# Input projection and paged sample attention as one stage of a hybrid decoder step

## The chip, the cores and the metric

One Trainium2 chip, one of its cores. The kernel is written engine by engine: TensorE (PE) multiplies, VectorE (DVE) and ScalarE (ACT) do elementwise work and reductions, GpSimd (POOL) does elementwise work and issues DMAs, SyncE (SP) issues DMAs. The program orders them by semaphores alone. The metric is the device time of one execution in microseconds (us); below 0.3% a difference can't be told from none.

## What is computed

One layer of a hybrid trunk in float32, for a prompt of 1040 tokens (16 meta tokens and 1024) and for 8 sample sequences of 4 new tokens each, with 4096 cached positions per sequence in 32 pages of 128.

```python
def mixer_inputs(h, ...):
    z = rms_norm(h, norm_w) @ w_in                       # 1024 -> 3600 columns
    dq, dk, dv, dg, gq, gk, gv, gg, ga = split(z)        # 512 512 512 512 256 256 512 512 16
    dq, dk = rms_norm(dq), rms_norm(dk)                  # per group of 64
    lg = log_sigmoid(ga @ gla_wa2 + gla_ba) / 16

def diff_attn_sample(...):                               # 8 sequences, 4 heads, 2 maps of 64
    kp, vp = cache_k[page_table], cache_v[page_table]    # 32 pages of 128 x 512 each
    a = softmax([q . kp + bias, q . k_new + bias])
    p = a[map 0] - lam * a[map 1]
    return p @ [vp, v_new]

def merge_out(...):
    mix = [rms_norm(o_d) * 0.8 * silu(dg), rms_norm(o_g) * silu(gg)]
    return h + mix @ w_out
```

Between the two stand causal differential attention over the prompt and a chunked gated linear attention (GLA), whose chunks of 128 tokens pass a state on.

## The kernel before

The tokens lie in 9 tiles: 8 of 128 rows and a last one of 64 rows, which holds the prompt's last 16 rows and the 32 sample rows. The program runs in five stages, each a block of its own with a barrier at its end, so that no instruction of one runs beside another stage.

**Projection** (lines 108 to 747). x is normed, turned by the PE and split into two fp32r parts (`xTh`, `xTl`), the weights likewise (`wh`, `wl`, on ACT and DVE); every product is three matmuls (hi*hi, lo*hi, hi*lo) over 8 slices of 128 input rows, 24 matmuls in a row. Columns are taken in 15 blocks of up to 256. For q, k, v, gv and both gates (dg, gg) a unit is one token tile: x is stationary, 256 weight columns move (`z_nat`, line 512), 108 units. For gq and gk (`z_turned`, line 524) the weights are stationary and 384, 384 or 320 tokens move: 12 units. q and k are then normed and turned; all of qT, kT, gqT, gkT, bT stay in SBUF. Values and gates go to DRAM.

**Paged sample attention** (lines 749 to 1148). For each sequence, 8 groups of 4 pages. SP loads keys into 4 slots (`load_keys`, line 817), POOL values into 8 (`load_values`, line 843): a page is 256 KB, fetched by a row number read from SBUF. The PE turns the keys 128x128 (line 925), ACT and DVE copy them out of PSUM, and the PE forms scores with a stationary of 32 queries' columns and 128 keys moving, four pages side by side in four column tiles of the array (line 940). Softmax, a turn of the probabilities (line 959), and products with 512 value columns, again in four column tiles (line 969).

**Prompt attention** (lines 1152 to 1636), then **GLA** (1640 to 2074), then the **output projection** (2077 to 2191), which again splits in two parts and adds the residual.

In GLA the loop over tiles is a ring of engines. For tile i+2 POOL forms exponents (`exponents`, lines 1894 to 1934) into one of two slots of `dd`, ACT takes exponentials (`decays`, line 1837), DVE multiplies (`factors`), the PE multiplies (line 1750), DVE masks and updates the state, ACT copies the outputs and takes norms, DVE applies norm and gate (`norm`, line 2048), the PE turns the result and ACT stores it to `mixT` (`mixed`, line 1873). POOL multiplies the gates by the norm weight (`gate`, line 1949), which needs only their load:

```python
for i in range(TILES):          # POOL
    if i + 2 < TILES:
        exponents(pool, linked, i + 2)
    gate(i)
```

ACT runs `decays(i + 2)`, `out(i)`, `turned_k(i + 1)`, `mixed(i - 1)` in this order.

## Time and profile before

| | us |
|---|---|
| median of 3 runs (1261.86, 1263.21, 1266.35) | 1263.21 |
| span of the profiled execution, first to last instruction | 1259.8 |
| until the first product of the projection | 18.65 |
| projection, to 418.5 | 399.85 |
| paged sample attention, to 816 | 397.5 |
| prompt attention, to 1021 | 205 |
| GLA and the start of the output projection, to 1178 | 157 |
| rest of the output projection | 81.8 |

The page gives no time of its own for the profiled execution besides its span; the span is 3.4 us under the median of the runs. "Busy" of the PE is modelled for pipelined matmuls, so the distance between starts tells the pace better than the length of one.

### The profile page before, as it was taken

What the parts mean: (1) busy time and instruction counts of PE and PEld (TensorE: products, weight loads), DVE (VectorE), ACT (ScalarE), POOL (GpSimd) and SP (SyncE); (2) the same over time, 40 slices, a digit from 0 to 9 for tenths busy, and PEclk for the clock granted to TensorE, in tenths of its full rate; (3) what the DMA queues carried; (4) which work ended last, traced back from release to release, by engine and by line L of the source; (5) the groups of instructions that cost most, each with busy time, mean ns of one, the idle gap of its engine ahead of it and who ended that gap; (6) DMA issues with size and microseconds to landing.
All of it is one profiled execution on the core that took longest, in us unless ns stands there. A gap on an engine that the chain in (4) does not pass through costs nothing. (4 is left out here: it accounts for less than half of the span.)

```text
span 1259.8 us, 27242 instructions
## 1 busy us (share of the span) xinstructions
PE 1038.3 (82%) x9055; PEld 868.5 (69%) x9055; DVE 584.6 (46%) x1430; ACT 490.0 (39%) x1383; POOL 254.2 (20%) x399
## 2 busy tenths in 40 slices
PE   4999999999999487879878887467788836777998
PEld 4999999997999466556655654155667625664886
DVE  4755522302222134443443443277878458868221
ACT  5644314613424223333333432156767345533110
POOL 0000000000000222343434341222211159800000
PEclk9999999999999799999999998558999967787999
DMA  5312332212111699999999999530000052102221
GB/s 169 93 38 95 106 122 80 82 34 76 53 49 49 215 386 338 385 387 387 387 387 387 387 387 169 148 111 9 17 10 13 1 175 74 51 26 69 97 89 60
DMA packets 106820, 195.21 MB, mean 155 GB/s; under 512 B 14406, under 2 KB 48652, under 8 KB 106732
## 3 DMA queue, kind: packets, MB, share of 16 engines
q1 hardware_dynamic: 85716, 126.03, 30.8%
q0 software_dynamic: 20480, 67.13, 14.3%
q8 instruction: 54, 0.88, 0.3%
q10 hardware_dynamic: 536, 0.89, 0.2%
q14 instruction: 34, 0.28, 0.1%
HBM read 174.41 MB, written 19.60 MB: 154 GB/s over the span
## 5 line engine op out<-in xcount | busy, mean ns | idle before, releaser
L843 POOL DMA_DIRECT2D vraw<-in_cache_v x256 | 137.6, 537 | 667.7 <-issue 663.8
L512 PE MATMUL pz<-wh,xTh 128*128 128x256 f32 (+1 forms) x864 | 248.7, 288 | 0.0
L512 PE MATMUL pz<-wh,xTl 128*128 128x256 f32 (+1 forms) x864 | 244.3, 283 | 0.0
L512 PE MATMUL pz<-wl,xTh 128*128 128x256 f32 (+1 forms) x864 | 244.2, 283 | 0.0
L925 PE MATMUL pk<-ident,kraw 128*128 128x128 f32 x1024 | 136.7, 291 | 57.0 <-DMA kraw<-in_cache_k 54.0
L925 PEld LDWEIGHTS pk<-ident,kraw 128*128 128x128 f32 x1024 | 121.8, 150 | 70.9 <-DMA kraw<-in_cache_k 62.0
L863 DVE COPY kt<-pk 128x512 f32<-128x512 f32 x128 | 82.9, 687 | 183.1 <-PE pk L925 182.1
L512 PEld LDWEIGHTS pz<-wh,xTh 128*128 128x128 f32 (+1 forms) x864 | 160.6, 186 | 1.6 <-issue 1.2
L512 PEld LDWEIGHTS pz<-wh,xTl 128*128 128x128 f32 (+1 forms) x864 | 160.7, 186 | 0.0
L512 PEld LDWEIGHTS pz<-wl,xTh 128*128 128x128 f32 (+1 forms) x864 | 160.5, 186 | 0.0
L643 DVE SCALAR_TENSOR_TENSOR wl<-wraw,nw,wh 128x256 fp32r<-128x256 f32 x112 | 52.3, 482 | 117.1 <-ACT wh L358 116.2
L861 ACT ACTIVATE kt<-pk 128x512 f32<-128x512 f32 x128 | 70.3, 595 | 80.0 <-PE pk L925 80.0
L1374 PE MATMUL pS<-ks,qs 128*128 128x512 f32 (+3 forms) x288 | 78.6, 426 | 10.0 <-DVE bl L1613 10.0
L969 PE MATMUL po<-vraw,pT 128*32 128x512 f32 x512 | 74.0, 652 | 11.3 <-DMA vraw<-in_cache_v 10.8
L940 PEld LDWEIGHTS psc<-kt,qq 128*32 128x32 f32 x2048 | 56.3, 110 | 39.1 <-issue 31.1
L940 PE MATMUL psc<-kt,qq 128*32 128x128 f32 x2048 | 72.2, 277 | 2.3 <-DVE kt L863 0.9
L1410 PE MATMUL pO<-vd,pT_b 128*128 128x128 f32 (+2 forms) x360 | 49.1, 310 | 22.8 <-ACT pT_b L1478 21.9
L1410 PEld LDWEIGHTS pO<-vd,pT_b 128*128 128x128 f32 (+2 forms) x360 | 39.7, 187 | 34.0 <-ACT pT_b L1478 22.9
L358 ACT ACTIVATE wh<-wraw,nw 128x256 fp32r<-128x256 f32 (+1 forms) x120 | 53.8, 484 | 23.8 <-PE pz L512 18.0
L871 ACT ACTIVATE sc<-psc 128x128 f32<-128x128 f32 x64 | 17.7, 277 | 115.4 <-PE psc L940 115.4
L2188 PE MATMUL pY<-woh,mh 128*128 128x512 f32 (+1 forms) x144 | 57.3, 398 | 5.7 <-DVE wol L2164 5.7
L1750 PE MATMUL pA<-ff 64*128 64x128 f32 (+1 forms) x264 | 27.5, 369 | 39.4 <-DVE at L2011 24.4
(241 smaller groups left out, 1857.5 us busy)
## 6 DMA issues: line engine op xcount, KB each, us to landing
kraw<-in_cache_k SPq DMA_DIRECT2D x256, 256.0 KB, 9.6
vraw<-in_cache_v POOLq DMA_DIRECT2D x256, 256.0 KB, 5.7
wraw<-in_w_in SPq DMA_DIRECT2D x14, 1024.0 KB, 5.6
out<-nat SPq DMA_DIRECT2D x32, 128.0 KB, 1.8
xb<-in_x_prompt SPq DMA_DIRECT2D x7, 512.0 KB, 3.6
xr<-in_x_prompt SPq DMA_DIRECT2D x7, 512.0 KB, 3.5
out<-xr SPq DMA_DIRECT2D x7, 512.0 KB, 2.6
val_d<-nat SPq DMA_DIRECT2D x16, 128.0 KB, 1.8
```

The lines of the kernel that those rows point to most:

```text
L358: act.activation(wh[:, c % 2, k, 0:n], wraw[:, c % 2, k, 0:n], ACT.Copy, scale=nw[:, k:k + 1])\
L512: ins = pe.matmul(z_at(u)[0:r, 0:CB], a[:, k, P * i:P * i + r], b[:, c % 2, k, :], start=(n == 0), stop=(n == 3 * KT - 1))
L643: dve.scalar_tensor_tensor(out=wl[:, c % 2, k, 0:n], in0=wraw[:, c % 2, k, 0:n], scalar=nw[:, k:k + 1], in1=wh[:, c % 2, k, 0:n].bitcast(F32),
L843: pool.dma_start(vraw[:, g % VR, n, :], cache_v.rearrange("a n p h d -> (a n) p (h d)")[bass.ds(page, 1)] .rearrange("o p c -> (o p) c")). ...
L861: ins = eng.activation(kt[:, g % 2, h, :], pk[h][:], ACT.Copy)
L863: ins = eng.tensor_copy(kt[:, g % 2, h, :], pk[h][:])
L925: ins = pe.transpose(pk[h][:, n * PAGE:(n + 1) * PAGE], kraw[:, g % KR, n, h * P:(h + 1) * P], ident[:])
L940: ins = pe.matmul(psc[g % 2][R * n:R * (n + 1), 0:PAGE], qq[:, 32 * h:32 * h + R], kt[:, g % 2, h, n * PAGE:(n + 1) * PAGE], start=(h == 0 ...
L969: ins = pe.matmul(po[R * n:R * (n + 1), :], pT[:, g % 2, R * n:R * (n + 1)], vraw[:, g % VR, n, :], start=(g == 0), stop=(n > 0 and g == G ...
L1374: return pe.matmul(pS[rows, s_at(u, m) + k0:s_at(u, m) + k1], typed(qs[:, i % 2, m, x, hh, 0:nq]), typed(ks[:, m, hh, k0:k1]), start=(x == ...
L1410: ins = pe.matmul(pO[q, hh * DV:(hh + 1) * DV], pT[0:kn, j, q], vd[0:kn, j, hh * DV:(hh + 1) * DV], start=(j == 0), stop=(j == i), tile_po ...
L2188: ins = pe.matmul(pY[2 * (i % 2) + n][0:r, :], a[:, i % 2, k, 0:r], b[:, k, n * 512:(n + 1) * 512], start=(k == 0 and x == 0), stop=(k == ...
```

## The change

The first two stages become one. Its steps are laid out by position: two positions to a unit of the projection, one after each half of its 24 matmuls.

- The cache is taken in 16 chunks of 16 pages (half a sequence), each with steps at positions base+0 to base+12. `base` is 40, 86, 94, 102, 111, 120 and on to 207. At step 0 the scores of the whole chunk; at steps 2 to 5 the keys of the next chunk are turned, group by group of 4 pages; at 3 to 6 the probabilities are turned; at 4 to 7 products with the values.
- Keys are turned by DVE in blocks of 32x32, 128x2048 at once, from SBUF to SBUF, in place of PE turns with copies out of PSUM. A score product has 32 rows of contraction and 32 stationary columns, so it takes a tile of 32x32 of the array; 512 keys move. 64 of them make a chunk, over all 16 tiles. The 2048 scores of a row stand in four PSUM banks; one maximum and one exponential take them all.
- `kraw` and `vraw` have 2 slots each (4 pages a slot), before 4 and 8. The weights have a ring of 11 slices of 128 rows, before two whole blocks.
- The gates dg and gg are projected as gq and gk are: weights stationary, tokens moving, 24 units in place of 36. DVE multiplies them by the norm weight, now a column per partition, as it evacuates them.
- qT, kT, gqT, gkT, bT and the gates go to DRAM and are loaded by the stages that read them.
- In prompt attention and GLA `norm` no longer applies the gate. POOL multiplies `mixT` by the gate after ACT has stored it there.
- The sample tile comes first in every block, since sample attention needs its q, k and v.

```diff
-            KR, VR = 4, 8
+            RW, RR = 11, 6
+            KR, VR = 2, 2
+            NCH, CG = 2 * NB, 4
...
+            base = [40, 86] + [94 + (87 * (c - 2)) // 10 for c in range(2, NCH)]
+            END = base[-1] + 13
...
+                def turn_keys(t):
+                    dve.wait_ge(k_in[t % KR], 64 * (t // KR + 1))
+                    if t // CG:
+                        dve.wait_ge(sc_done, t // CG)
...
+                    dve.transpose(kx[:, GRP * g:GRP * g + GRP, :].rearrange("p n x -> p (n x)"),
+                                  kraw[:, t % KR, :, :].rearrange("p n x -> p (n x)")).then_inc(kx_done, 1)
...
+                def scores(c):
+                    pe.wait_ge(kx_done, CG * (c + 1))
...
+                    for j in range(4):
+                        for i in range(4):
+                            rows = slice(32 * i, 32 * i + 32)
+                            for h in range(H):
+                                ins = pe.matmul(pS[32 * h:32 * h + 32, 512 * i:512 * i + 512],
+                                                qz[rows, c // 2 % 2, h, j, :],
+                                                kx[rows, :, P * h + 32 * j:P * h + 32 * j + 32],
+                                                start=(j == 0), stop=(j == 3), tile_position=(32 * i, 32 * h))
...
+                def load_keys(t):
+                    if t >= KR:
+                        sp.wait_ge(kx_done, t - KR + 1)
...
+                for t in range(NG):
+                    if t >= VR:
+                        pool.wait_ge(pv_done, pv_no[((t - VR) // CG, (t - VR) % CG)] + 1)
...
+                    if u < NU:
+                        half_unit(u, range(0, KT // 2))
+                    cache_steps(2 * u)
+                    if u < NU:
+                        half_unit(u, range(KT // 2, KT))
+                    small_steps(u)
+                    cache_steps(2 * u + 1)
...
                 def gate(i):
                     r = rows_of(i)
+                    m = mixT[:, H:2 * H, P * i:P * i + r]
                     pool.wait_ge(vg_in[i % 2], 32 * (i // 2 + 1))
-                    g = gg[0:r, i % 2, :].rearrange("p (h d) -> p h d", h=H)
-                    pool.tensor_tensor(g, g, gw[0:r, :].unsqueeze(1).to_broadcast([r, H, DV]), ALU.mult)\
-                        .then_inc(ggd, 1)
+                    pool.wait_ge(mgo, i + 1)
+                    pool.tensor_tensor(m, m, gg[:, i % 2, :, 0:r], ALU.mult).then_inc(ggd, 1)
...
                     if i + 2 < TILES:
                         exponents(pool, linked, i + 2)
-                    gate(i)
+                    if i >= 1:
+                        gate(i - 1)
+                gate(TILES - 1)
```

The PE, at the start of the paged stage before. `pk` takes turned keys, `psc` scores:

```order
L917 UNCONDITIONAL_BRANCH [waits barrier_Pool_Activation_PE_DVE_SP_release]
L925 MATMUL pk<-ident,kraw 128x128 [waits k_in0]
L925 MATMUL pk<-ident,kraw 128x128 x15
L940 MATMUL psc<-kt,qq 32x128 [waits kt_act,qq_done]
L940 MATMUL psc<-kt,qq 32x128 x3
L940 MATMUL psc<-kt,qq 32x128 [waits kt_act]
```

The PE now, around the scores of the second sequence's first chunk, in the middle of a v unit (line 797; `pS_c` takes scores):

```order
L797 MATMUL pz<-wl,xTh 128x256
L898 MATMUL po<-vn,pT 32x512 [waits vn_done,pt_act]
L854 MATMUL pS_c<-kx,qz_c 32x512 [waits exp_done,qz_done,kx_done]
L854 MATMUL pS_c<-kx,qz_c 32x512 x63
L797 MATMUL pz<-wh,xTh 128x256
```

No key is turned on the PE any more, and the paged products stand between halves of units, so whatever they wait for, the projection behind them waits for too.

POOL in GLA before, from the end of one tile's exponents to the next tile's (`gg` is the gate tile):

```order
L1932 COPY dd<-bT 128x256
L1933 TENSOR_SCALAR dd<-dd 128x512
L1949 TENSOR_TENSOR gg<-gg,gw 128x512 [waits vg_in0]
L1900 TENSOR_TENSOR dd<-bT 128x256 [waits dexp]
L1901 TENSOR_TENSOR dd<-bT 128x256
```

And now:

```order
L2018 COPY dd<-bT 128x256
L2019 TENSOR_SCALAR dd<-dd 128x512
L2036 TENSOR_TENSOR mixT<-mixT,gg 128x4x128 [waits mgo,vg_in0]
L1986 TENSOR_TENSOR dd<-bT 128x256 [waits dexp]
L1987 TENSOR_TENSOR dd<-bT 128x256
```

The instruction between two tiles' exponents now also waits for `mgo`, which ACT raises at the end of `mixed` of the tile before.

SP in the new stage, between two stores of gq units (line 457) with a block of page loads between (each page is a read of its number, two address steps and the DMA):

```order
L457 DMA gqT_d<-stg 128x384 [waits stg_act]
L409 TENSOR_LOAD pages [waits kx_done]
L409 ISA x2
L410 ISA
L410 DMA kraw<-in_cache_k 128x512
```

SP's page loads wait for a turn on DVE, and stores of the projection are queued behind them.

## Rows read from the trace of the kernel before

**Rows 1.** Windows by stage: length, engines' busy time (count), PE clock, DMA share, GB/s
```profile
18.65:418.50 399.85, 396.03 (x3160) 381.85 (x3158) 143.14 (x371) 159.16 (x460) 0.00 (x0) 1.00 0.24 75
418.50:816.00 397.50, 301.71 (x3819) 211.58 (x3818) 155.86 (x510) 123.00 (x355) 137.59 (x256) 0.91 0.98 343
816.00:1021.00 205.00, 152.92 (x1045) 122.92 (x1045) 143.94 (x271) 130.85 (x363) 38.38 (x27) 0.88 0.09 26
1021.00:1178.00 157.00, 105.98 (x675) 87.31 (x676) 116.15 (x240) 62.54 (x181) 78.05 (x111) 0.78 0.26 85
```

**Rows 2.** Timeline, projection's PE: start us, busy us, line, operation; then line 524 whole
```profile
344.98 0.28 PE L512 MATMUL pz<-wh,xTh 128*128 128x256 f32 x1
345.10 0.28 PE L512 MATMUL pz<-wh,xTl 128*128 128x256 f32 x1
...
L524 PE MATMUL pz<-xTh,wh x96: 306/334/338, 246.5 to 293.5; 128*128 128x384 f32 x64, 128*128 128x320 f32 x32
```

**Rows 3.** Timeline of the PE in the paged stage
```profile
560.89 1.13 PE L999 MATMUL ppt<-osb,selc 128*128 128x128 f32 x8 [1.33 <-DVE selc L1109]
561.85 1.91 PE L925 MATMUL pk<-ident,kraw 128*128 128x128 f32 x16
...
566.09 1.39 PE L940 MATMUL psc<-kt,qq 128*32 128x128 f32 x32 [0.15 <-ACT kt L861]
...
571.07 1.06 PE L969 MATMUL po<-vraw,pT 128*32 128x512 f32 x8
571.95 0.29 PE L940 MATMUL psc<-kt,qq 128*32 128x128 f32 x4
```

**Rows 4.** PE in GLA, products of 64 rows and of 128 rows, with their windows
```profile
1035.76 3.85 PE L1750 MATMUL pA<-ff 64*128 64x128 f32 x32 [15.02 <-DVE ff L1977]
1036.00:1039.50 3.50, 3.50 (x32) 2.97 (x32) 3.47 (x5) 0.00 (x0) 3.50 (x5) 0.50 1.02 408
...
1053.95:1055.20 1.25, 1.25 (x8) 1.25 (x8) 1.25 (x3) 1.25 (x4) 1.17 (x3) 0.50 0.00 0
1054.34 0.63 PE L1774 MATMUL pOg<-state_p,qz 128*128 128x128 f32 x2
1054.77 0.63 PE L1771 MATMUL pOg<-vg,at 128*128 128x128 f32 x2
```

**Rows 5.** Page issues on SP and POOL; two DMA groups with KB and us to landing
```profile
422.51 47.06 SPq L817 DMA_DIRECT2D kraw<-in_cache_k  x38
608.37 0.54 POOL L843 DMA_DIRECT2D vraw<-in_cache_v  x1 [0.70 <-issue]
gd<-gate_d SPq DMA_DIRECT2D x8, 256.0 KB, 2.7
xr<-in_x_prompt SPq DMA_DIRECT2D x7, 512.0 KB, 3.5
```

**Rows 6.** Timeline, long DVE instructions of prompt attention
```profile
1002.77 1.24 DVE L1560 TENSOR_REDUCE sm<-pS 128x1 f32<-128x1040 f32 x1 [6.17 <-PE pS L1374]
1008.51 0.76 DVE L1579 TENSOR_SCALAR e<-e,inv 128x1040 f32<-128x1040 f32 x1
```

**Rows 7.** Timeline of ACT and POOL in GLA
```profile
1024.96 0.64 POOL L1900 TENSOR_TENSOR dd<-bT 128x256 f32<-128x256 f32 x1 [0.85 <-DVE dd L1933]
1029.75 1.51 POOL L1933 TENSOR_SCALAR dd<-dd 128x512 f32<-128x512 f32 x1
1053.53 0.69 POOL L1900 TENSOR_TENSOR dd<-bT 128x256 f32<-128x256 f32 x1
1062.43 1.27 POOL L1949 TENSOR_TENSOR gg<-gg,gw 128x512 f32<-128x512 f32 x1
1063.49 2.71 ACT L1837 ACTIVATE ff<-dd 128x512 f32<-128x512 f32 x5 [3.58 <-DVE state_p L2035]
1069.69 0.59 ACT L1873 ACTIVATE mixT<-pM 128x512 f32<-128x512 f32 x1
1074.33 2.71 ACT L1837 ACTIVATE ff<-dd 128x512 f32<-128x512 f32 x5 [4.05 <-DVE state_p L2035]
```

1834 lines of the change are left out of this document (947 added, 887 removed).

## Prediction, written before the changed kernel ran

> **What bounds the kernel now.** First the windows by stage [rows 1]. In the projection the PE is busy for 396 of 399.85 us at full clock, while the DMA engines are busy for 0.24 of the time and DVE and ACT for 143 and 159 us. In the paged stage it is the reverse: the DMA share is 0.98 at 343 GB/s, and the PE's 302 busy us are filled from gaps. The two stages need different resources, 400 us of PE and about 390 us of DMA, and a barrier keeps them apart. Laid over each other they could at best take about the longer of the two sums. The other stages come after and aren't relieved.
>
> Next the pace of the PE. A product of 256 columns starts every 0.12 us, so a unit of 24 takes 2.88 us; line 524 places 95 steps of three products between 246.5 and 293.5, 0.495 us each, 3.96 us a unit [rows 2]. In the paged stage 16 turns take 1.91 us, four score groups of 32 instructions 1.39, and two groups of value instructions (8, for one group of pages) 0.88 from start to start [rows 3].
>
> **The merged stage, part by part.** *Projection.* Its own work stays, but for the gates: 36 units of 2.88 (103.7 us) become 24 of 3.96 (95.0). 399.85 - 103.7 + 95.0 = 391.2 us, after 18.65 us of start.
>
> *Scores.* 64 products per chunk, each two instructions as all float32 products here. Four column tiles side by side run in the time of one: the value group of four such products has 512 columns and takes 0.88 us [rows 3]. Without any overlap of row groups a chunk would be 16 x 0.88 = 14.1 us; with all four row groups together 3.5 us. Do row groups overlap? GLA has products of 64 rows that alternate between the halves of the array: 16 in 3.85 us, 0.24 each, at clock 0.50. Products of 128 rows at the same clock come every 0.43 us [rows 4]. So two row groups give 1.8 times. A floor is issue: 32 instructions in 1.39 us less the last one's tail of 0.16 are 0.039 each, so 128 take 5.0 us. I take 5.0, since both kinds of overlap have a row; the ends are 3.5 and 14.1.
>
> The Trainium skill, "TensorE: Matmul & The Clock Gate", Part 3, says that 16 tiles of 32x32 with 512 columns ran 10.6 times as fast as one by one. By it a chunk would take, as an estimate, 64 x 0.88 / 10.6 = 5.3 us if one product alone takes the 0.88, and the sum would be 5 us higher; no run here shows it. Against the change speaks "TensorEngine Tiling", Key Properties: changing the tiling mode drains the engine. About 12 changes a chunk at the tail of 0.2 us that a lone product has would be 2.4 us, or 30 us more in all than I add below. The trace agrees only weakly: the score product behind the value group starts 0.88 us after it, with no visible gap [rows 3].
>
> *The rest of a chunk on the PE*: 16 turns of probabilities 1.9; four value groups 3.5; every second chunk new keys, 8 output products and small ones, about 4 us (by 0.039 to 0.14 us an instruction [rows 3]), so 2 on average; 0.6 for changes between shapes (from 0 to 2.4). With the scores 13.0 us, 16 chunks 208 us. PE turns of keys and copies out of PSUM are gone. The bias products add 3.
>
> *Keys on DVE.* No row shows a 32x32 turn of 128x2048. Reductions take 1.24 us and a multiplication 0.76 for 1040 elements [rows 6], so 1.5 to 2.4 us. I take 2.3, near the reduction, since a turn is no plain multiplication: 64 of them are 147 us, and the maxima 16 x 2.7 = 43. With the projection's 143, DVE is at half load. It is not the bound, but it is a link, since SP loads a key group only when the one two before is turned.
>
> *Loads.* SP issues a page every 1.24 us (38 in 47.06), POOL too (0.54 and 0.70 idle) [rows 5]. So a group of four pages takes 5.0 us to issue and about 2.7 to land [rows 5], and with two slots the third group of a chunk can be asked for only when the first is used. Values: group 2 lands 7.7 us after the first group's product. The PE is there two positions later, each 1.44 or 1.98 (half a unit) + 0.5 (turns) + 0.9 (values): 5.7 or 6.8. Group 3 lands at 12.6 against 8.5 or 10.1. The PE waits about 4.1 us a chunk in units of 256, 2.5 in those of 384. Keys: DVE ends its third turn 11.7 us and its fourth 16.7 us after the first begins, where the PE needs 8 to 10 us for these positions. In gate units the PE waits for DVE at the next unit but one, and gets about 4 us behind. The stores, queued on SP behind 16 page issues (19.8 us a chunk), have slots for two to three units and just hold. Together 4.5 us a chunk, 15 chunks: 67.5 us (ends 0 and 150). The first keys cost 6, weight slices that meet a waiting DVE at block changes 10, the end with its barrier 3.
>
> Sum: 18.65 + 391.2 + 208 + 3 + 67.5 + 6 + 10 + 3 = 707 us, where before the two stages ended at 816. From chunk 1 on the mean period is about 33 us for 8.4 MB, 250 GB/s, so DMA is no longer a bound.
>
> **The later stages.** *Prompt attention* now loads qT and kT first: 0.4 us of issue and 3.5 to land for 512 KB [rows 5], about +4 (between 0 and 6). The last gate now follows `mixed` on POOL: +1.3, as one of 1.27 does in GLA [rows 7]. Inside, POOL's `split_lo` has time enough. DVE's shorter `norm` gains perhaps 0.5 us a tile beside other waits; I count nothing.
>
> *GLA* gets a new ring. Before, POOL is ahead with `exponents`. Now its `gate(i - 1)` waits for `mixed(i - 1)`, ACT's last step of loop i, and behind it is queued `exponents(i + 3)`, for which ACT's first step of loop i+1 (`decays`) waits. Price: from the start of `decays` to the end of `mixed` 1063.49 to 1070.28, 6.8 us; gate 1.27; exponents 8.9 us beside a busy DVE (1053.53 to 1062.43) or 6.3 alone (1024.96 to 1031.26); hops 0.2 [rows 7]. That is 14.6 to 17.2 us a loop against 10.84 now (1063.49 to 1074.33). Four loops at +5 are 20; the last tile, of half width, about 1. The last tile's loads wait for a gate instead of a norm: 3.5; the last gate 1.3. Together +26 (16 to 32). The shorter `norm` runs beside `decays` and gains nothing.
>
> The output projection doesn't change. So 707 + (1259.8 - 816) + 31.5 = 1182 us of span. With the 3.4 us by which the median of the runs lies above the profiled span: **1186 us**, 6% faster.
>
> **Rivals.** *A, one tile of rows at a time.* If the 32-row groups do not overlap, scores cost 14.1 a chunk: 16 x 9.1 = 146 us more, 1332, slower than before. For it: no row has 32-row groups, or four at once. Against: 1.8 times at two halves [rows 4]. It decides from 77/16 = 4.8 us more a chunk, 9.8 us for the scores. *B, lockstep.* PE waits for DVE and for values add up rather than overlap, 10 us a chunk in place of 4.5, from the late fourth turn (6) and the late fourth group (4.1): +82, 1268. For it: every engine is strictly in order, and SP's queue serves keys, stores and weights. Against: a PE that waits gives the others time, and scores of 5 us stand between. *C, waits vanish.* If landing is quicker and slots suffice, 67.5 + 6 + 10 fall to about 10: 1112. For it: the DMA engines are half idle. Against: the issue alone takes 5 us a group. *D, the ring in GLA doesn't close*: -21 us, 1165; this lies in the forecast's own range. A lower PE clock in waits (0.91 in the paged stage [rows 1]) would push from the forecast to B.
>
> **How the numbers follow.** Forecast with D 0.60 (1135 to 1235), C 0.17, B 0.14, A 0.09. What differs from before by less than 0.3%, 4 us, can't be told from none. The range is 1110 to 1250: it leaves out A and the worse half of B, about 0.16. Faster: 0.60 + 0.17 + half of B, 0.84. Within 0.3%: 0.03 out of B. Slower: A and the rest of B, 0.13.
>
> **What would show it.** In the profile after: scores of a chunk about 5 us from first to last start; a chunk's period 28 to 36 us; PE waits of 2 to 5 us before the third and fourth value group, released by DMA, and before gate units, released by DVE; keys turned in 64 DVE instructions of 1.5 to 2.4 us; end of the merged stage near 707; no DMA share above 0.8 for long. In GLA `decays` 14.6 to 17.2 us apart, waiting for POOL. Wrong would be scores near 14 us, DVE turns over 4 us, or waits of 10 us a chunk.

## The result: 2.6% slower, and the profile of the kernel after

The changed kernel takes **1297.05 us** (median of 4 runs, 1293.48 to 1302.13), the kernel before 1264.78 us beside it (4 runs, 1261.86 to 1268.85). The ratio is 1.0255, 95% interval 1.0221 to 1.0289: 32 us slower, where 1186 us was forecast, 6% faster. The profiled run is the longest of the four, with a span of 1300.4 us at a mean granted clock of 0.873. Of serial_rows, below, one of four executions (1408.78 us) was slow, with a lower granted clock than the others; its median leaves it out, but its trace is of that one.

A marker common to all kernels here is SyncE's first load of prompt attention, which follows the end of the stage before: at 816.17 us before, 821.14 us after. So the merged stage, forecast to end at 707, is no shorter than the two that it replaces. By windows, answering to [rows 1] (columns: window, length, busy us and instructions of each engine, granted PE clock, DMA share, GB/s):

```profile
18.65:90.00 71.35, 57.00 (x412) 53.70 (x411) 40.72 (x107) 36.65 (x114) 4.54 (x8) 0.88 0.52 148
90.00:134.00 44.00, 3.49 (x30) 3.28 (x28) 9.98 (x8) 2.14 (x7) 0.00 (x0) 0.58 0.76 85
134.00:820.60 686.60, 580.88 (x5670) 439.99 (x5670) 282.86 (x417) 201.84 (x513) 133.03 (x248) 0.92 0.69 230
820.60:1031.00 210.40, 155.80 (x1037) 125.98 (x1037) 138.65 (x266) 127.61 (x347) 35.75 (x25) 0.86 0.19 61
```

Two things stand out. For 44 us, from 90 to 134, TensorE is busy for 3.5 us and the other engines for 10 at the most, yet the DMA engines are busy for 0.76 of the time and move only 85 GB/s. And in the 687 us after it TensorE is idle for 106 us. Who it waits for is told by the view of waits, TensorE, whole merged stage (columns: engine, tile, line, released by; us in total, times, longest):

```profile
PE po L893 <- DMA vraw<-in_cache_v: 76.3, 21, 5.7
PE ptb L813 <- DVE nat L1019: 41.0, 1, 41.0
PE pS_c L761 <- DVE xTl L979: 10.2, 4, 6.0
```

The one wait of 41.0 us names VectorE's line 1019. That is only the last link. What VectorE did then is in its timeline (start us, busy us, line, operation; in brackets the idle time before it and who ended it):

```profile
89.03 0.42 DVE L1019 TENSOR_TENSOR nat<-tmp,qwr 128x256 f32<-128x256 f32 x1
116.99 4.51 DVE L1071 STREAM_TRANSPOSE kx<-kraw 128x2048 f32<-128x2048 f32 x2 [27.53 <-DMA skew<-kx]
126.35 2.31 DVE L1071 STREAM_TRANSPOSE kx<-kraw 128x2048 f32<-128x2048 f32 x1 [4.85 <-DMA kraw<-in_cache_k]
130.76 2.31 DVE L1071 STREAM_TRANSPOSE kx<-kraw 128x2048 f32<-128x2048 f32 x1 [2.10 <-DMA kraw<-in_cache_k]
133.00 0.38 DVE L998 TENSOR_REDUCE rms<-tmp 128x4 f32<-128x256 f32 x1
```

Ahead of the first key turn `turn_keys(0)` waits for `band_st`: the buffer `band` (the relative biases, 384 values for each of 4 heads) lies inside `kx`, and its skewed copies must be in DRAM before keys overwrite it. The four DMAs that store them, 192 KB each, take this long (DMA issues, median us from issue to landing at the end):

```profile
skew<-kx SPq DMA_DIRECT2D x4, 192.0 KB, 19.8
```

Two windows of the changed kernel during this read:

```profile
90.00:100.00 10.00, 3.49 (x30) 3.28 (x28) 0.00 (x0) 2.14 (x7) 0.00 (x0) 0.85 0.88 27
100.00:110.00 10.00, 0.00 (x0) 0.00 (x0) 0.00 (x0) 0.00 (x0) 0.00 (x0) 0.50 0.88 29
```

My sum had no term for this store. The trace of before had a row to show for it: there the store lay behind the last key load, beside the last sample, and a window there reads

```profile
770.00:780.00 10.00, 6.82 (x81) 4.04 (x79) 6.17 (x29) 2.43 (x7) 1.07 (x2) 0.95 0.88 33
```

The same DMA share, 0.88, with 33 GB/s. Next to the paged stage's 0.98 with 343 GB/s [rows 1] this is a transfer of another kind, and it was there to be seen. Nor was it free there. The three value pages that GpSimd asks for beside it (DMA issues of before, window 763 to 779) land after 22.3 us in the median, where that of all is 5.7, and TensorE waits for values (window 740 to 816), which it did not do from 600 to 740:

```profile
vraw<-in_cache_v POOLq DMA_DIRECT2D x3, 256.0 KB, 22.3
```

```profile
PE po L969 <- DMA vraw<-in_cache_v: 10.8, 4, 4.8
```

What went about as forecast: a chunk's scores, 128 instructions in 4.46 us in 13 of the 16 chunks (timeline of TensorE; two chunks took 5.25, and one 5.71 at a granted clock of 0.73), and the key turns of 2.3 us (groups by line: busy us, mean ns, idle before).

```profile
388.92 4.46 PE L854 MATMUL pS_c<-kx,qz_c 32*32 32x512 f32 x128
```

```profile
L1071 DVE STREAM_TRANSPOSE kx<-kraw 128x2048 f32<-128x2048 f32 x64 | 147.1, 2305 | 174.3 <-DMA kraw<-in_cache_k 145.3 <-DMA skew<-kx 27.5 <-DVE stg L1047 1.1
```

And the later stages: from the marker to the end of the span 479.3 us, 475.3 forecast. The linear attention's loop: ScalarE's squares of the nine tiles begin 111.2 us apart, 13.9 a loop.

```profile
L1951 ACT ACTIVATE squares_g<-og x36: 292/293/311, 1063.3 to 1174.5; 128x128 f32<-128x128 f32 x32, 64x128 f32<-64x128 f32 x4
```

Landing times answer to [rows 5], where 2.7 us for 256 KB was read:

```profile
kraw<-in_cache_k SPq DMA_DIRECT2D x256, 256.0 KB, 4.7
vraw<-in_cache_v POOLq DMA_DIRECT2D x256, 256.0 KB, 5.2
```

### The profile page after: what moved, and what is told of

Read it like the earlier page. It is cut to its first block and busy times, and to the rows that moved or that the text cites. A ratio compares the mean times of both kernels' runs of the same rounds, so it can differ in the third digit from the quotient of the medians.

```text
span 1300.4 us, 23647 instructions
## 1 busy us (share of the span) xinstructions
PE 997.4 (77%) x8207; PEld 785.9 (60%) x8207; DVE 610.6 (47%) x1078; ACT 448.3 (34%) x1202; POOL 242.4 (19%) x398
## 5 line engine op out<-in xcount | busy, mean ns | idle before, releaser
L1071 DVE STREAM_TRANSPOSE kx<-kraw 128x2048 f32<-128x2048 f32 x64 | 147.1, 2305 | 174.3 <-DMA kraw<-in_cache_k 145.3
L797 PE MATMUL pz<-wh,xTh 128*128 128x256 f32 (+1 forms) x576 | 180.1, 313 | 0.0
L797 PE MATMUL pz<-wh,xTl 128*128 128x256 f32 (+1 forms) x576 | 170.8, 297 | 0.0
L797 PE MATMUL pz<-wl,xTh 128*128 128x256 f32 (+1 forms) x576 | 170.0, 295 | 0.0
L893 PE MATMUL po<-vraw,pT 128*32 128x512 f32 x512 | 82.0, 706 | 76.9 <-DMA vraw<-in_cache_v 76.3
L797 PEld LDWEIGHTS pz<-wl,xTh 128*128 128x128 f32 (+1 forms) x576 | 114.2, 198 | 0.0
L793 PE MATMUL pz<-xTh,wh 128*128 128x384 f32 (+1 forms) x288 | 103.0, 358 | 3.9 <-DVE wl L986 3.2
L793 PE MATMUL pz<-xTl,wh 128*128 128x384 f32 (+1 forms) x288 | 96.3, 334 | 0.0
L793 PE MATMUL pz<-xTh,wl 128*128 128x384 f32 (+1 forms) x288 | 96.0, 333 | 0.2 <-issue 0.2
L854 PE MATMUL pS_c<-kx,qz_c 32*32 32x512 f32 x2048 | 74.2, 607 | 0.0
L793 PEld LDWEIGHTS pz<-xTh,wh 128*128 128x128 f32 x288 | 56.7, 197 | 15.8 <-issue 10.1
```

What stands on the lines that cost most here:

```text
L793: ins = pe.matmul(z[:, 0:tn], b[:, w, m * P:m * P + P], a[:, k, t0:t0 + tn], start=(n == 0), stop=(n == 3 * KT - 1))
L797: ins = pe.matmul(z[0:r, 0:CB], a[:, k, P * x:P * x + r], b[:, w, :], start=(n == 0), stop=(n == 3 * KT - 1))
L854: ins = pe.matmul(pS[32 * h:32 * h + 32, 512 * i:512 * i + 512], qz[rows, c // 2 % 2, h, j, :], kx[rows, :, P * h + 32 * j:P * h + 32 * j ...
L893: ins = pe.matmul(po[32 * n:32 * n + 32, :], pT[:, v % 2, 32 * n:32 * n + 32], vraw[:, t % VR, n, :], start=(g == 0), stop=(g == CG - 1 an ...
L1071: dve.transpose(kx[:, GRP * g:GRP * g + GRP, :].rearrange("p n x -> p (n x)"), kraw[:, t % KR, :, :].rearrange("p n x -> p (n x)")).then_i ...
```

## The experiments

Each edit is made to the changed kernel unless said otherwise; times are medians, each beside runs of the kernel before on the same chip, whose medians lay between 1264.79 and 1265.88 us. "Marker" is the start of prompt attention as above, SyncE's first load of kT, read in the one traced execution of each run. It is not sharp: gla_gate_late changes nothing before it, and its marker is 7.5 us earlier than that of the changed kernel. Nor is the changed kernel's median: its four executions lie between 1293.48 and 1302.13.

| run | us | against the changed kernel | ratio to before, 95% | marker |
|---|---|---|---|---|
| changed kernel | 1297.05 | | 1.0221 to 1.0289 | 821.1 |
| band_apart | 1294.10 | -3.0 | 1.0195 to 1.0246 | 809.0 |
| band_wide | 1271.75 | -25.3 | 1.0036 to 1.0076 | 789.9 |
| first_keys | 1260.34 | -36.7 | 0.9946 to 0.9988 | 785.0 |
| no_values | 1217.76 | -79.3 | 0.9592 to 0.9669 | 735.6 |
| no_keys | 1253.90 | -43.2 | 0.9867 to 0.9933 | 774.9 |
| no_loads_wide | 1151.51 | -145.5 | 0.9052 to 0.9134 | 672.2 |
| no_chunks | 915.17 | -381.9 | 0.7194 to 0.7246 | 437.8 |
| serial_rows | 1376.99 | +79.9 | 1.0823 to 1.0997 | |
| gla_gate_late | 1269.54 | -27.5 | 1.0004 to 1.0066 | 813.7 |
| values_apart | 1258.93 | -38.1 | 0.9919 to 0.9986 | 777.9 |
| pages_ahead | 1281.35 | -15.7 | 1.0068 to 1.0144 | 802.7 |
| half_values | 1267.09 | -30.0 | 0.9973 to 1.0020 | 787.3 |
| keys_apart | 1289.74 | -7.3 | 1.0169 to 1.0233 | 811.8 |
| steps_apart | 1172.74 | -124.3 | 0.9213 to 0.9300 | 721.5 |
| steps_tuned | 1164.12 | -132.9 | 0.9182 to 0.9239 | 710.6 |

### The store of the bias rows: who waits, or what it does to the queues

```
-            band = flat_k[0:H, 6144:6528]
+            band = pr[0:H, 0:384]
...
+                    if c == 0:
+                        act.wait_ge(band_st, 16 * H)
...
-                    elif t == 0:
-                        dve.wait_ge(band_st, 16 * H)
```

> The skewed bias rows that go to DRAM are kept in the buffer of the probabilities instead of the buffer of the turned keys, so the first chunk's key turns no longer wait for that store; the store itself is as before. Theory 1 (the wait of VectorE for the store, 27.5 us, is what stops TensorE for 41 us between units 14 and 15): the stop shrinks to under 10 us and the time falls by 30 to 41 us, to 1256 to 1267. Rival (the store fills the DMA queues, whoever waits for it): the first two groups of keys are turned at once, groups 2 and 3 land only after the store, TensorE still stops for 25 to 35 us, and the time falls by under 12 us.

Measured: 1294.10 us, 3 us under the changed kernel and within its spread, and a stop of 36.3 us in place of 41.0. The first two groups of keys are turned at once, and then VectorE stands just as long, for keys:

```profile
85.83 4.50 DVE L1071 STREAM_TRANSPOSE kx<-kraw 128x2048 f32<-128x2048 f32 x2
118.13 2.31 DVE L1071 STREAM_TRANSPOSE kx<-kraw 128x2048 f32<-128x2048 f32 x1 [27.80 <-DMA kraw<-in_cache_k]
```

The rival holds: the wait that the profile names was not the cause. How the store stops TensorE is told by SyncE: the keys do not land late, they are asked for late (timeline of SyncE in band_apart, then its reads of page numbers: shortest, median and longest in ns):

```profile
82.06 13.16 SPq L505 DMA_DIRECT2D skew<-pr  x4
95.27 7.33 SPq L457 DMA_DIRECT2D qT_d<-stg  x1
110.46 13.23 SPq L410 DMA_DIRECT2D kraw<-in_cache_k  x11
```

```profile
L409 SPq TENSOR_LOAD <-pages x256: 262/268/7342, 57.1 to 749.9; - x128
```

The four issues of the store take SyncE 13.16 us and the issue behind them 7.33, where 0.4 is usual, and the read of the first page number takes 7.3 us where 0.27 is usual. The first key page is asked for at 110.46 only, and the pages then land 3 us after their issue. So the store holds up whoever issues behind it on SyncE. That it holds up another queue too is shown by GpSimd's value pages in the kernel before, above.

So the store itself. Its source is one partition for each head, read 128 times. In band_wide four products with the bias column repeated 128 times make the rows on all 128 partitions, and each row is stored once:

```
-                    pe.matmul(pS[0:H, 1024:1024 + 384], relb, oh, start=True, stop=True).then_inc(rel_done, 1)
+                    for h in range(H):
+                        ins = pe.matmul(pS[:, 512 * h:512 * h + 384], relx[:, h, :], oh, start=True, stop=True)
+                    ins.then_inc(rel_done, 1)
...
-                            sp.dma_start(skew[h:h + 1].rearrange("o (q x) -> o q x", q=P),
-                                         band[h:h + 1, :].unsqueeze(1).to_broadcast([1, P, 384])).then_inc(band_st, 16)
+                            sp.dma_start(skew[h].rearrange("(q x) -> q x", q=P),
+                                         band[:, h, :]).then_inc(band_st, 16)
```

> As band_apart, and the four skewed copies are stored from 128 partitions (one row of 384 each, made by four products of 128 columns and one addition on VectorE) instead of from one partition each; same bytes in DRAM. Theory (the 27 us of the store at 27 to 29 GB/s come from its source, one partition for each 192 KB): the store lands in under 8 us, TensorE stops for under 10 us there, and the time falls by 35 to 45 us against the changed kernel, to 1252 to 1262. Rival (the rows of 1536 bytes in DRAM are what is slow): the store still takes 25 us or more and the time is that of band_apart.

Measured: 1271.75 us, 25.3 less. The same bytes land in 2.1 us instead of 19.8 (DMA issues of band_wide), and SyncE issues all four in 1.95 us instead of 13.16:

```profile
skew<-pr SPq DMA_DIRECT2D x4, 192.0 KB, 2.1
```

The width of the source was the cause, not the rows in DRAM, which are the same. The time expected was 1252 to 1262; it missed by 10 us, because a stop of 13.4 us is left at the same place (TensorE's waits of band_wide):

```profile
PE ptb L816 <- DVE nat L1024: 13.4, 1, 13.4
```

The rest of that stop is the order of the first four key turns: all in unit 13, the last two for pages that are asked for only then. In first_keys, which is band_wide with this edit, they are one per unit:

```
-                    if u == 13:
-                        for t in range(KR, CG + KR):
-                            load_keys(t)
+                    if 13 <= u < 13 + CG:
+                        load_keys(u - 13 + KR)
...
-                    if u == 13:
-                        for t in range(CG):
-                            turn_keys(t)
+                    if 13 <= u < 13 + CG:
+                        turn_keys(u - 13)
```

> band_wide with the first chunk's four key turns, and the loads they release, one per unit from unit 13 on instead of all four inside unit 13. Theory (the 13.4 us for which TensorE still stops there come from VectorE waiting 16 us for groups that only SyncE's next issues bring, with the norm of the unit queued behind): the stop goes under 4 us and the time falls by 8 to 14 us, to 1258 to 1264. Rival: the wait moves on to the first scores (unit 20) and the time stays within 4 us of 1272.

Measured: 1260.34 us (10 runs), 11.4 less than band_wide; TensorE's waits for line 1023, the same step there, are 4.6 us in three pieces. The time is as the theory had it, the stop just over its 4 us.

### What the waits for pages cost

In no_values all value loads but those of the first two groups are left out, in no_keys the same for keys, in no_loads_wide both, with band_wide's store:

```
-                for t in range(NG):
+                for t in range(VR):
...
-                        pe.wait_ge(v_in[t % VR], 64 * (t // VR + 1))
+                        pe.wait_ge(v_in[t % VR], 64)
...
                 def load_keys(t):
+                    if t >= KR:
+                        return
...
-                    dve.wait_ge(k_in[t % KR], 64 * (t // KR + 1))
+                    dve.wait_ge(k_in[t % KR], 64)
```

> Value pages are loaded for the first two groups of the 64 only, and all products use these: 62 of 64 value loads (16.3 MB) are left out, so the time is that of a kernel without waits for values. Theory (TensorE's waits for values, 76.3 us in the profile, are on the path): the merged stage gets 60 to 90 us shorter, the time falls to 1205 to 1240. Rival (the waits only take the place of others, for keys on VectorE, which come next): it falls by under 30 us, to 1267 or more.

> Key pages are loaded for the first two groups of the 64 only, and all turns read these: 62 of 64 key loads (16.3 MB) and their 248 issues on SyncE are left out. Theory (VectorE's 145 us of waits for keys stand in front of the weight splits and the norms that TensorE needs): the time falls by 30 to 60 us beside the store of the bias rows, which stays. Rival (turned keys are early enough, three half units ahead of the scores, and the waits of VectorE cost TensorE nothing): it falls by under 15 us, to 1282 or more.

> The bias rows stored from 128 partitions (as band_wide) and only the first two groups of key and of value pages loaded, the rest left out: what the merged stage takes without waits for pages. If the four costs add (26 us for the store, 79 for values, 43 for keys), the time is 1149, a merged stage of about 672 us. If the projection and the chunks' own work on TensorE are the rest, and forecast rightly (391 + 208 + 3 + 19), the stage ends near 640 and the time is 1117. If over 1170, keys and values waits hid each other and a further cost, not named yet, lies in the stage.

(A page is 256 KB, so what is left out is 65 MB for values and as much for keys; the 16.3 MB that I wrote are wrong by a factor of four, the forecasts don't rest on them.)

Measured: -79.3, -43.2 and -145.5 us. The parts alone, 25.3 + 79.3 + 43.2 = 147.8, add up to the 145.5 of all three, and 1149 forecast by adding meets 1151.5. The sum counts the changed kernel's median three times and is no sharper than some us each time, but the costs don't hide one another to a large extent. Granted clock and traffic with and without loads, same start (windows from 337 us, first the changed kernel, then no_loads_wide):

```profile
337.00:820.00 483.00, 406.12 (x3907) 293.03 (x3905) 189.29 (x246) 135.17 (x308) 104.06 (x194) 0.92 0.71 241
```

```profile
337.00:672.00 335.00, 315.34 (x3261) 229.51 (x3260) 154.48 (x200) 116.72 (x269) 0.00 (x0) 0.97 0.13 42
```

The 43 us of the keys are remarkable, since hardly a wait of TensorE names keys. In no_keys its waits for *values* are 54.0 us instead of 76.3, and values land in 3.6 us instead of 5.2:

```profile
PE po L895 <- DMA vraw<-in_cache_v: 54.0, 21, 4.3
PE ptb L815 <- DVE nat L1021: 33.9, 1, 33.9
```

Read by the waits, 22 of the 43 us would go through the shared DMA engines, 7 more through the stop at unit 14. That is not shown as a cost, and the sum above speaks against it: these 29 us would be gone with the values' loads and the store as well, and the three together would give 119, not 145.5. In no_values TensorE's other waits grow by some 15 us, which may be waits for keys that the waits for values had covered. Whether the rest goes through VectorE was tried by moving only the key turns (and the loads behind them) from 2, 3, 4, 5 half units behind the scores to 2, 3, 5, 7:

> The changed kernel with one thing moved: the key turns of the next chunk (and the load of the group two further on) stand 2, 3, 5 and 7 half units behind a chunk's scores instead of 2, 3, 4 and 5. Theory (the 43 us of the keys come through VectorE, which stands waiting for pages with weight splits and norms queued behind): VectorE's 145 us of waits for keys fall below 110 and the time falls by 10 to 25 us, to 1272 to 1287. Rival (they come through bandwidth and issues): within 6 us of the changed kernel, 1291 to 1303.

```
-                        if 2 <= d <= 5 and c + 1 < NCH:
-                            turn_keys((c + 1) * CG + d - 2)
+                        if d in (2, 3, 5, 7) and c + 1 < NCH:
+                            turn_keys((c + 1) * CG + (2, 3, 5, 7).index(d))
```

Measured: 1289.74, -7.3 (1288.90 to 1292.76, just under the changed kernel's lowest). VectorE's waits for keys fall from 145.3 to 88.9 us, and that brings 7: most of what VectorE waits isn't on the path. The value lies just outside both expectations, nearer to the rival.

### What makes a value wait long

> The changed kernel with one thing moved: the value groups of a chunk, and the turns of their probabilities, stand two half units of the projection apart instead of one (at 4, 6, 8 and 10 half units behind the scores). Theory (a slot's refill of some 10 us, four issues of 1.24 and a landing of 5.2, is waited for only because the slot is needed again two half units later; TensorE's 76 us of value waits go with the distance): the waits for values fall under 15 us in all and the time falls by 50 to 80 us, to 1217 to 1247. Rival (the loads are late by bandwidth, all queues share 241 GB/s here): the waits stay over 50 us and the time falls by under 20.

```
-                        if 4 <= d <= 7:
-                            values(c, d - 4)
-                        if 3 <= d <= 6:
-                            turn_probs(c, d - 3)
+                        if d in (4, 6, 8, 10):
+                            values(c, (d - 4) // 2)
+                        if d in (3, 5, 7, 9):
+                            turn_probs(c, (d - 3) // 2)
```

Measured: the value waits are all but gone, 8.2 us in place of 76.3, as the theory said. The time falls by 38.1 only, between the two expectations: new waits stand in the projection, for VectorE's gates and weight splits (3.9 us before in all, 24.8 now).

```profile
PE pz L793 <- DVEq L1050: 14.3, 5, 7.3
PE pz L793 <- DVE wl L986: 10.5, 2, 6.2
PE pS_c L761 <- DVE xTl L979: 10.3, 4, 6.1
PE ptb L820 <- ACTq L658: 9.5, 7, 5.1
PE po L893 <- DMA vraw<-in_cache_v: 8.2, 7, 2.9
```

> The changed kernel with one thing moved: GpSimd reads the four page numbers of a value group into registers before it waits for the slot, not one by one between the four issues. Theory (of the 10 us of a refill, four steps of 1.24 us, 0.70 us each are the register loads): each waited-for refill is 2.8 us shorter, two per chunk in a row, so the time falls by 25 to 45 us, to 1252 to 1272. Rival (the queue's own issue, 0.54 us, and the landing set it, register loads overlap them): under 10 us.

```
-                    if t >= VR:
-                        pool.wait_ge(pv_done, pv_no[((t - VR) // CG, (t - VR) % CG)] + 1)
-                    for n in range(GRP):
-                        page = pool.value_load(...)
+                    of = [pool.value_load(...) for n in range(GRP)]
+                    if t >= VR:
+                        pool.wait_ge(pv_done, pv_no[((t - VR) // CG, (t - VR) % CG)] + 1)
+                    for n in range(GRP):
```

Measured: -15.7, between the two expectations. Waits for values are 50.6 us instead of 76.3; the register loads count, for less than the theory had.

> From the third group on only the first half of each value row is loaded (1 KB instead of 2 KB), with the same number of issues and of rows; the other half of the values is left as it was. Theory (issues and distance set the value waits, bytes little): the landing falls from 5.2 to 3.5 to 4.5 us and the time falls by 10 to 30 us. Rival (bandwidth sets them): the waits for values more than halve and the time falls by over 45 us, to under 1252.

```
+                        cols = W if t < VR else W // 2
-                        pool.dma_start(vraw[:, t % VR, n, :], page_rows(cache_v, page)).then_inc(v_in[t % VR], 16)
+                        pool.dma_start(vraw[:, t % VR, n, 0:cols], page_rows(cache_v, page)[:, 0:cols]).then_inc(v_in[t % VR], 16)
```

Measured: -30.0, at the edge of the theory's span. The landing is 4.0 us instead of 5.2, the waits 50.8:

```profile
vraw<-in_cache_v POOLq DMA_DIRECT2D x248, 128.0 KB, 4.0
```

Half the bytes bring 30 us, so bytes are not little, as the theory had it; but the waits don't more than halve, as the rival had it. A refill thus consists of register loads, issues and landing, and the first and the last were each shown to be worth something; what turns it into a wait is the distance of two steps to the slot's next use. One chunk shows it. TensorE's value groups (timeline; third and fourth group have their waits in brackets), then GpSimd's issues for the third:

```profile
441.82 1.21 PE L893 MATMUL po<-vraw,pT 128*32 128x512 f32 x6
...
453.78 1.06 PE L893 MATMUL po<-vraw,pT 128*32 128x512 f32 x8 [2.08 <-DMA vraw<-in_cache_v]
460.10 1.93 PE L893 MATMUL po<-vraw,pT 128*32 128x512 f32 x8 [3.29 <-DMA vraw<-in_cache_v]
```

```profile
444.28 0.54 POOL L543 DMA_DIRECT2D vraw<-in_cache_v  x1 [17.82 <-issue]
445.42 0.54 POOL L543 DMA_DIRECT2D vraw<-in_cache_v  x1 [0.61 <-issue]
446.58 0.54 POOL L543 DMA_DIRECT2D vraw<-in_cache_v  x1 [0.62 <-issue]
447.73 0.54 POOL L543 DMA_DIRECT2D vraw<-in_cache_v  x1 [0.61 <-issue]
```

The slot is free at 443.03, the last of four pages is issued at 448.27, and the product starts at 453.78: 10.75 us for a refill, 5.5 of it landing.

### The projection alone, and the scores' order

> The bias rows from 128 partitions as in band_wide, and every cache step left out (page loads, key turns, scores, probabilities, values, sample outputs): the projection with its transposed gates alone, then the later stages as they are. Forecast by the prediction's terms: 18.65 + 391 + 19 (bias, first keys' and weights' shares) = 420 to 430, time 890 to 910; the chunks of no_loads_wide (stage end 672) would then cost 15.2 to 15.7 each where 13.0 was forecast. If the projection itself is what was under-costed, the stage ends at 445 or later and the chunks cost 14 or less.

```
-                return [(c, pos - base[c]) for c in range(NCH) if 0 <= pos - base[c] <= 12]
+                return []
...
-                sp.wait_ge(od_st, 16 * NB)
+                sp.dma_start(od_d.rearrange('t (a x) -> t a x', a=2), nat[0:NS, 0:2, :]).then_inc(od_st, 16)
+                sp.wait_ge(od_st, 16)
```

Measured: 915.17 us, marker 437.8. The units of transposed gates come every 3.95 us on average (340.61 to 388.05 for twelve), as forecast. But the nine units with the gate logarithms, beside which short products share the one bank `ptb`, take 4.8 us where the units after them take 2.9: seven of them wait for ScalarE to read the bank. In the kernel before, where these products go to `pz`, the same nine take 4.0 us each (line 549, 306.66 to 338.75), so 0.7 a unit is new, some 6 us in all.

```profile
292.46 0.69 PE L820 MATMUL ptb<-wa,gaT 17*128 17x256 f32 x2 [1.02 <-ACTq L656]
297.28 0.69 PE L820 MATMUL ptb<-wa,gaT 17*128 17x256 f32 x2 [0.63 <-ACTq L656]
```

And the start is slow: from 18.65 to 60 us TensorE is busy for 29.4 us at a clock of 0.83, where before it was busy for 37.5 at full clock. The first product of the third block of columns starts at 102.38, before at 86.86: 15.5 us later.

> The scores' 64 products of a chunk are issued row group by row group, so that only the four products of one row group (the four column groups) can run side by side, not sixteen; same products, same sums. Theory (the order as written lets row groups overlap, which is why a chunk's scores take 4.9 us and not the 14.1 us of four times as many columns in a row): the scores take 9 us more per chunk, 16 times, and the time rises by 100 to 150 us, to 1397 to 1447. Rival (column groups alone give the overlap, row groups add nothing): no change, 1292 to 1302.

```
-                    for j in range(4):
-                        for i in range(4):
-                            rows = slice(32 * i, 32 * i + 32)
+                    for i in range(4):
+                        rows = slice(32 * i, 32 * i + 32)
+                        for j in range(4):
```

Measured: +79.9 us. A chunk's scores last 9.1 us instead of 4.46 at full clock, in 11 of the 16 chunks (timeline of serial_rows):

```profile
652.40 9.13 PE L854 MATMUL pS_c<-kx,qz_c 32*32 32x512 f32 x128
```

The direction is the theory's, the size isn't: 80 us, below its 100 to 150, since a chunk with four column groups alone takes 9.1 us and not my upper bound of 14.1. 16 x 4.7 is 75, near the 80.

### The ring in the linear attention

> In the gated linear attention GpSimd does the gate of tile i-2 after the exponents of tile i+2, instead of that of tile i-1, and the gates have four buffers and loads of their own, so that neither GpSimd nor the loads of the values wait for the end of tile i-1. Theory (the stage's 31 us more come from a ring: gate of i-1 needs the mix of i-1, the exponents of i+3 queue behind it on GpSimd, ScalarE's decays wait for them, 41 us in the profile): the stage takes 15 to 31 us less and the time falls to 1266 to 1282. Rival (GpSimd's own work per tile, exponents and gate, is the bound): the stage gets less than 8 us shorter.

Besides the lines below, the gates get four buffers in place of two and semaphores of their own, so the loads of the values no longer wait for a gate.

```
-                    if i >= 1:
-                        gate(i - 1)
+                    if i >= 2:
+                        gate(i - 2)
+                gate(TILES - 2)
                 gate(TILES - 1)
```

Measured: -27.5 us (10 runs). The squares of the nine tiles, 111.2 us apart before, are 87.5 apart now, 10.9 a loop, which is the kernel before's pace:

```profile
L1953 ACT ACTIVATE squares_g<-og x36: 292/293/311, 1057.2 to 1144.7; 128x128 f32<-128x128 f32 x32, 64x128 f32<-64x128 f32 x4
```

ScalarE's 41.1 us of waits for GpSimd's exponents, of which this row of the changed kernel tells, are 6.0 us now.

```profile
ACT ff L1923 <- POOL dd L2019: 41.1, 7, 7.7
```

The ring was real, and the gate one loop later with its buffers breaks it; which of the two it takes isn't told apart. The stage gained 23.7 us; the few more in the total are within this kernel's own spread (1262.91 to 1276.68).

### All of it together

> A version that computes everything: bias rows from 128 partitions; first four key turns one per unit instead of all in one; value groups of a chunk two half units apart instead of one, key turns 2, 3, 5 and 7 half units behind the scores instead of 2 to 5; the four page numbers of a value group read into registers before the wait; the gate of the linear attention as in gla_gate_late. Theory (value waits come from a slot that is refilled in 10 us while its next use is two half units, 6 to 8 us, away): over half of the 79 us of the values and some of the 43 of the keys go; 1297 - 26 - 20 - 45 - 20 = 1185, range 1160 to 1225. Rival (the loads are short of DMA bandwidth, not of time between steps): the value waits move and stay, time 1235 or more.

The edits are those of band_wide, first_keys, values_apart, keys_apart, pages_ahead and gla_gate_late.

Measured: 1172.74 us, ratio 0.9257 (0.9213 to 0.9300) to the kernel before. TensorE's waits for values are 4.8 us in all; the longest are now for key turns:

```profile
PE pS_c L859 <- DVE kx L1074: 14.4, 6, 7.1
```

The gain of 124.3 us is near the sum of its parts run alone: 36.7 (first_keys) + 38.1 + 15.7 + 27.5 + 7.3 (keys_apart) = 125.3. That they meet to 1 us is luck: each part is taken against the changed kernel's one median, and values_apart alone leaves only 8.2 us of waits for values, of which pages_ahead could hardly take 15.7. So the sum does not prove the parts independent.

> steps_apart, with SyncE's page numbers of a key group also read ahead of the wait for the slot, and the last key turn 6 half units behind the scores instead of 7 (TensorE waited 14.4 us in 6 times for a turn in steps_apart). Theory (key refills are waited for like value refills): the waits of the scores go, VectorE's waits for keys fall from 69 to under 50 us, time 1155 to 1168. Rival (SyncE's register loads delay the stores and weight slices behind them as before, and the last turn at 6 waits for its page instead): within 4 us of 1173.

```
+                    of = [sp.value_load(...) for n in range(GRP)]
                     if t >= KR:
                         sp.wait_ge(kx_done, t - KR + 1)
...
-                        if d in (2, 3, 5, 7) and c + 1 < NCH:
+                        if d in (2, 3, 5, 6) and c + 1 < NCH:
```

Measured: **1164.12 us** (1163.77 to 1164.75), 8.6 less again, ratio 0.9211 (0.9182 to 0.9239). The time is within the theory's range, but VectorE still waits 68.9 us for keys, so the expected fall of that wait didn't come; TensorE's waits for key turns fell from 14.4 to 9.7. Both edits were made at once and aren't told apart. The DMA engines now move more beside the projection: 274 GB/s in the stage at a clock of 0.97 (window from 337 us of steps_tuned).

```profile
337.00:711.00 374.00, 342.75 (x3534) 248.72 (x3518) 169.42 (x221) 124.19 (x285) 92.56 (x172) 0.97 0.80 274
```

## Why the prediction was wrong

The marker of each run splits the merged stage, and the forecast's terms can be laid beside it:

| part | forecast | measured | from |
|---|---|---|---|
| start, projection, biases, end (18.65 + 391.2 + 3 + 3) | 416 | 437.8 | no_chunks |
| 16 chunks, first keys, weight slices (208 + 6 + 10) | 224 | 234.4 | no_loads_wide less no_chunks |
| waits for pages, keys and values | 67.5 | 117.8 | band_wide less no_loads_wide |
| store of the bias rows | 0 | 31.2 | changed kernel less band_wide |
| sum | 707 | 821.1 | |
| later stages | 475.3 | 479.3 | |

By size the waits for pages come first, 50 us over the forecast, then the store with 31, the projection with 22, the chunks with 10 and the later stages with 4. The "measured" column is of single traced executions, and the changed kernel's was 5 us over its median.

1. **The missing term, 31 us (25 in the medians).** The step that failed here is the count of what is moved, in which the store stood at nothing. The prediction counted page loads, stores of q, k and gates on SyncE's queue, but not the store of the skewed biases, which the merge carries from the end of the paged stage, where only GpSimd's last value pages ran beside it, to the 12th unit, ahead of the first keys. What the runs put in its place: four DMAs from one partition each, 27 to 29 GB/s, DMA engines kept busy, and SyncE, which issues keys, held up at its next issues. TensorE stands, and its granted clock is 0.50, the lower level of 1.2 GHz, in the second of the two windows above.

The Trainium skill, "SBUF — State Buffer", Door 1: The DMA port swizzle, says that the bandwidth goes with the number of SBUF ports that the partitions reach, 27.2 GB/s each, and that partitions 0 to 3 share one. The four rows of `band` lie just there; by it, as an estimate, 786 KB take 28.9 us. The trace agrees: 27 to 29 GB/s in the windows, 31.4 us from the first issue (85.61) to the end of VectorE's wait for the store (116.99), and landings of 2.1 us from 128 partitions. That the port is what sets the rate, and not something else about a source of one partition, no run here tells apart. I had read that page's subject as one of big tiles and did not apply it to a small tensor that is read 128 times.

2. **Waits for pages, 118 where 67.5 stood, the largest miss.** For values the mechanism was right: TensorE waits ahead of the third and fourth value group, released by DMA; the chunk in the timeline above has 5.4 us of it, the mean is 4.8 (76.3 in 16), and 2.5 to 4.1 were forecast. Mis-sized is the landing, 2.7 us taken from a 256 KB load in a quiet stage [rows 5], 5.2 measured. With it a refill is 10.75 us, not 7.7; part of that cost nothing, since TensorE came for the slot 8.7 us after it was free, where 5.7 stood. The step that failed is the keys: little of the 4.5 us a chunk was theirs, and leaving out their loads brings 43.2 us. "DMA is no longer a bound" was true of the mean, 241 GB/s at a share of 0.71, and wrong as a reason for a short landing: leaving out the keys alone brings values to 3.6 us. A wait may also cost more than its length: the clock is at 0.92 in this stage and at 0.97 without loads.

3. **The projection, 22 us more.** The gates' price (95 us) holds. Not counted: the slower first phase, 15.5 us up to the third block of columns, and one PSUM bank for all short products, with which the nine units of the gate logarithms take 4.8 us each where they took 4.0 before, some 6 us. In the first phase of no_chunks TensorE waits 10.6 us for VectorE's split of x (`xTl`), before 3.5. Why VectorE is later, and why TensorE's clock is at 0.83 from 18.65 to 60 us, where before it was at 1.00, no run here takes apart.

4. **Chunks, 14.7 us each where 14.0 stood** with first keys and slices. The scores are the term that I had put the most doubt into, and with 4.46 against 5.0 it held; the floor of issue under it was no floor, since 127 steps from start to start take 3.88 us, 0.031 each and not 0.039. Rival A, no overlap of row groups, was priced at 14.1 us a chunk; serial_rows shows 9.1.

By the 10.6 times of the Trainium skill, "TensorE: Matmul & The Clock Gate", Part 3, the prediction estimated 5.3 us; the trace's 4.46 is shorter. The drain at a change of tiling mode that the Trainium skill, "TensorEngine Tiling", Key Properties, tells of would by the prediction's estimate have made 30 us more. The chunks as a whole are 10 us over their term and the scores in no_loads_wide 7 us under theirs, so if the other terms held some 17 us of it could be there; no run shows the drain by itself.

5. **The linear attention** nearly as forecast: 13.9 us a loop, just under the 14.6 to 17.2, and 31 us more from its start to the end of the kernel against 26. **Prompt attention** starts its score products 6 us later behind the marker than before, where 4 stood. Rival D, the ring doesn't close, is out by this and by gla_gate_late; rival C, the waits vanish, by the 118 us.

6. **Rival B**, lockstep, with 10 us a chunk and 1268 us, comes nearest to the mechanism: 7.4 us of page waits a chunk. Its reason, VectorE's late fourth turn in front of TensorE, is not borne out: moving the key turns brought 7 us. The range, 1110 to 1250, failed since the missing term was outside every case: without the store, at 1271.75, the time is still 22 us above the range, so the waits for pages and the projection's 22 us would have missed it too. No case let several terms be high at once.

So where did the overlap go? No part of it failed to overlap. TensorE's own work in the merged stage ends at 672 us with no page to wait for (no_loads_wide), 144 us before the old stages' end. Of these 144 us, 149 are given back: 118 to pages that come too late for their step, 31 to a small store put ahead of everything. Neither belongs to the overlap itself: with the bias rows stored from 128 partitions, the steps placed further apart and the ring in the linear attention opened, the same change is 100 us faster than the kernel before (1164.12 against 1264.79).

## What to carry to other kernels

When stages are merged, list every DMA that changes its place, the small ones too, and look in the trace of before for windows in which the DMA share is high while the GB/s are low: such a transfer holds up what is issued behind it, little at the end of a stage (here 10.8 us of waits) and much in front of one that lives on loads (a stop of 41). Size a double-buffered load by its refill time under the new traffic (register load, issue and landing, as measured with all queues running), and put the uses of a slot further apart than that. A wait's releaser is where to begin, not where to end: here taking away the named wait brought 3 us at the most, taking away the slow store behind it 25.

## What the runs showed of the hardware that I had not expected

- A store of 4 x 192 KB from one partition each runs at 27 to 29 GB/s and keeps the DMA engines at a share of about 0.88. Beside it an issue on SyncE takes up to 7.3 us in place of 0.4 and the read of a page number up to 7.3 in place of 0.27 (band_apart), and value pages from GpSimd land after 22 us in place of 5.7 (kernel before). From 128 partitions each of the four lands in 2.1 us.
- Products of 32 rows and 32 columns with all sixteen positions in turn: 64 products of 512 float32 columns in 4.46 us at full clock; with only the four columns side by side 9.1 us.
- Key pages that no wait of TensorE names cost 43 us; among other things they make value pages land in 5.2 instead of 3.6 us, at 241 GB/s and a share of 0.71, far from full.
- Reading four page numbers into registers before a wait instead of between the issues is worth 16 us in 62 refills.
